# Modulation sums over partitions: quarters of the array, streamed, gathered by the group and turned once

## The chip, the cores and the metric

The kernel runs on one core of a Trainium2 chip. The metric is device time in microseconds of one execution, from the first to the last instruction with what the device adds around them; lower is better. Everything is fp32 at the interface. The engines are PE (matrix multiply), DVE (vector), ACT (activation), POOL (GpSimd) and SP, which issues the DMAs. Each engine works its own instructions in program order and waits on semaphores.

## The reference, cut to what matters

```python
for i in range(DEPTH):                       # DEPTH = 2, D_MODEL = 1024, 512 latent + 256 context tokens
    mx = (silu(c)     @ ada_w[i] + ada_b[i]).reshape(B, 1, 9, D_MODEL)   # for the latent tokens
    mc = (silu(c_ctx) @ ada_w[i] + ada_b[i]).reshape(9, D_MODEL)         # for the context tokens
    x   = x   + 0.5 * mx[2] * swiglu(modulate(rms_norm(x,   g), mx[0], mx[1]), w_gu, w_down)
    ctx = ctx + 0.5 * mc[2] * swiglu(modulate(rms_norm(ctx, g), mc[0], mc[1]), w_gu, w_down)
    ...                                      # i = 0: pooling and neighbourhood attention; i = 1: RG-LRU
    x   = x   + mx[5] * yx
    x   = x   + 0.5 * mx[8] * swiglu(modulate(rms_norm(x, g), mx[6], mx[7]), w_gu, w_down)
```

The change concerns the first two lines: two vectors of 1024 (silu of c and of c_ctx) times a matrix of 1024 x 9216 for each of the two layers. The 18432 results are the shifts, scales and gates of all stages that follow, for latent and for context tokens.

## The kernel before

The residual stream lies in SBUF with the channels on the partitions (8 tiles of 128 channels, 768 tokens in a row). Matmuls keep a 128x128 tile of a weight matrix in the array and stream the tokens. Each product is made of three passes: high part of the weights times high and low part of the tokens, low part times high. SP loads a weight panel (`raw`), ACT makes its high part (`w_hi`, L771), POOL the low one (`w_lo`, L661); there are two buffers of each, and a buffer is free when its panel has been used (`panel_used`).

An FFN f has two halves h. Stage `gu{f}{h}` makes gate and up products: 11 rounds of two panels (8 k-tiles each), into the PSUM tiles `pair_a` and `pair_b`, whence ACT takes silu and DVE makes g (L1090 to L1096). Stage `dn{f}{h}` multiplies g with `w_down`: 8 panels of 11 k-tiles, in turn into `pair_a` and `pair_b`, and DVE adds each, times its gate `mod_g`, to `resid` (L1121). Stages whose output is normed next (dn01, dn11 among them) end in a `tail` in which the last two panels are done by halves of the tokens. The order of the stages is gu00, dn00, gu01, dn01, then projections and attention, gu10, dn10, gu11, dn11, gu20, dn20, gu21, dn21, the recurrent block, and FFN 3.

The modulation is spread over these stages. The matrix is cut into 72 chunks of 256 columns. The first 8 are done in the prologue. The other 64 are done one by one: 11 in each of gu00, gu01, gu10, gu11 (one a round), 4 in each of dn00, dn01, dn10, dn11 and dn20 (one for every two panels). A chunk q goes like this:

- SP loads 1 MB of `ada_w` into `ada_raw` when the sums of chunk q-1 are done (`load_ada`, L508).
- DVE multiplies its 8 k-tiles with the two condition vectors and adds them up (`sum_ada`, L1056 and L1060, 16 instructions on 128x256), v = 0 for c and v = 1 for c_ctx. What is left is a sum over the 128 partitions of `ada_sum`.
- PE makes it (`use_ada`, L1648): for each tile t of 128 columns and each v the 128x128 block of `ada_sum` is the stationary operand and a column of ones the moving one. The result is one column of `pair_c`, with the channels already on the partitions.
- DVE adds the bias and stores two columns for each v in `mods` (`take_ada`, L1074). `mods_done` counts the chunks.

In a down stage DVE's order is: mod_g for the stage (`coef_g`, L1046), and then for each k from 0 to 7 `sum_ada` if k is even or `take_ada` if it is odd, the wait for panel k, the update of `resid`. PE calls `use_ada` behind panel 0, 2, 4 and 6. No scheduler is at work; the order on each engine is that of the code.

Of the kernel before, what the change touches and what calls it, by code (L numbers as in the profile page):

```python
# [91 lines left out]
HALF = T // 2  # L92
LEFT = 512 - HALF


def trunk(nc, x, c, ctx_in, c_ctx, ada_w, ada_b, norm_g, w_gu, w_down, ab_in, ab_out, pool_w,
# [51 lines left out]
    with ExitStack() as stack:  # L148
# [40 lines left out]
        ident = sb("ident", [P, P])  # L189
        ones = sb("ones", [P, P])  # L190
        rg_scale = sb("rg_scale", [P, 2 * KR])
        rg_tanh = sb("rg_tanh", [P, 2 * KR])
# [9 lines left out]
        acc = sb("sum_sq", [P, T])  # L202
        ada_sum = sb("ada_sums", [P, 2, 2 * P])

        def alias(start, end):
# [102 lines left out]
        ada_used = sem("ada_used")  # L308
        mods_done = sem("mods_done")
        coef_done = sem("coef_done")  # L310
        rows_landed = sem("rows_landed")
# [70 lines left out]
        def sums_before(q):  # L382

            return (q - ADA0) * (2 * KD)

        def ada_seen(q):
# [262 lines left out]
        def _(pool):  # L649
# [4 lines left out]
            nc.gpsimd.affine_select(out=ident[:, :], in_=ident[:, :], compare_op=ALU.not_equal, fill=1.0, base=0,  # L654
                                    pattern=[[-1, P]], channel_multiplier=1).then_inc(const_done, 1)

            def low(p, par, kt):
# [372 lines left out]
        def _(dve):  # L1030
# [32 lines left out]

            def sum_ada(q):

                dve.wait_ge(ada_landed, (q - (ADA0 - 1)) * 16)
                sum_tiles(lambda k: ada_raw[:, k, :], [ada_sum[:, v, :] for v in range(2)], ada_summed, sums_before(q))

            def take_ada(q):

                dve.wait_ge(ada_used, q - (ADA0 - 2))
                src = pC[:, 0:4].rearrange("p (t v) -> p v t", v=2)
                for v in range(2):
                    last = nc.vector.tensor_tensor(mods[:, ds(q * 2, 2), v], src[:, v, :], cols[:, ds(q * 2, 2)], ALU.add)  # L1074
                last.then_inc(mods_done, 1)

            def gate_up(f, h):
                W = SEQ if f == 3 else T
                p0, F0 = first[f"gu{f}{h}"], GU_BEFORE[f, h]
                q0 = ada_first.get(f"gu{f}{h}")  # L1080
                with dve.Fori(0, KC) as i:
                    if q0 is not None:
                        sum_ada(i + q0)
# [12 lines left out]
                    nc.vector.tensor_tensor(gl[:, ds(i, 1), 0:W].rearrange("p o n -> p (o n)"), gbuf[:, 0, 0:W],  # L1096
                                            gh[:, ds(i, 1), 0:W].rearrange("p o n -> p (o n)").bitcast(F32),
                                            ALU.subtract).then_inc(g_split_done, 1)
                    if q0 is not None:
                        take_ada(i + q0)  # L1100

# [28 lines left out]
            def outputs(name, p0):  # L1130

                site = SITE[name]
                if name[:2] != "dn" or name[3] == "0":
                    dve.wait_ge(mods_done, ada_seen((shift_tile(site) + 3 * KD) // 2 - 1))
# [3 lines left out]
                for k in range(KD - 2 if name in NORM_AT else KD):  # L1138
                    if q0 is not None:
# [72 lines left out]
            def tail(name, p0, q0):  # L1212

                i = NORM_AT[name]
                if q0 is not None:
                    sum_ada(q0 + KD // 2 - 1)
                dve.wait_ge(tail_mm, 2 * (i - 1) + 1)
# [6 lines left out]
                statistics(name, 0)  # L1224
                if q0 is not None:
                    take_ada(q0 + KD // 2 - 1)
                dve.wait_ge(panel_used, p0 + KD - 1)
# [14 lines left out]
                rows_of(name, 1, 0, KD)  # L1242
                if name == "dn01":
                    pad_tokens()

# [53 lines left out]


            dve.wait_ge(cols_t, 1)
            nc.vector.tensor_copy(cols[:, :], pR[:, 0:ROWS]).then_inc(cols_done, 1)
# [281 lines left out]
        def _(pe):  # L1584
# [56 lines left out]

            def use_ada(q):

                pe.wait_ge(ada_summed, sums_before(q + 1))
                pe.wait_ge(mods_done, q - (ADA0 - 1))
                for t in range(2):
                    for v in range(2):
                        last = nc.tensor.matmul(pC[:, 2 * t + v:2 * t + v + 1], ada_sum[:, v, t * P:(t + 1) * P],  # L1648
                                                ones[:, 0:1], start=True, stop=True)
                last.then_inc(ada_used, 1)  # L1650

            def gate_up(f, h, after):
                W = SEQ if f == 3 else T
                p0, F0 = first[f"gu{f}{h}"], GU_BEFORE[f, h]
                q0 = ada_first.get(f"gu{f}{h}")
                if after is not None:

                    first_panels(p0, after, W, W)
                    if q0 is not None:
                        use_ada(q0)  # L1660
                with pe.Fori(int(after is not None), KC) as i:
# [12 lines left out]
                    if q0 is not None:  # L1674
                        use_ada(i + q0)

            def outputs(name, p0, kt, hi, lo, start=0, each=None):
                W = SEQ if name in X_ONLY else T
                q0 = ada_first.get(name)
                with pe.Fori(start, KD // 2 - int(name in NORM_AT)) as i:  # L1680
                    for r in range(2):
                        pe.wait_ge(split_ready, i * 2 + (p0 + r + 1))

                        pe.wait_ge(resid_done, i * 2 + (UPD[name] + r - 1))
                        panel(pair[r], r, kt, hi, lo, W, each)
                        if q0 is not None and r == 0:
                            use_ada(i + q0)
                if name in NORM_AT:
# [21 lines left out]
            def tail(name, p0, kt, hi, lo, q0):  # L1710
# [12 lines left out]
                if q0 is not None:  # L1723
                    use_ada(q0 + KD // 2 - 1)
                half_panel(of[0], 0, kt, hi, lo, b, width(name), then(sum_rows, sum_at)).then_inc(panel_used, 1)
                half_panel(of[1], 1, kt, hi, lo, b, width(name), then(spread_rows, spread_at)).then_inc(panel_used, 1)

            def last_tile(n):
# [261 lines left out]
```

## Time and profile before

| | us |
|---|---|
| median of 3 runs (lowest, highest) | 2880.06 (2879.87, 2881.6) |
| profiled execution | 2877.64 |
| its span in the profile | 2875.9 |
| PE busy | 2719.7 (95%) |
| DVE busy | 1487.4 (52%) |
| ACT busy | 768.7 (27%) |
| POOL busy | 891.1 (31%) |
| mean granted clock of PE | 0.968 of full speed |

The span is what the profiler sees from the first to the last instruction; the profiled execution's own time is 1.7 us more. PE's matmuls overlap, and a record's length includes the way through the array, so the distance between two starts says more than the length of one record. An fp32 matmul shows as two records, the matmuls of the split products as one each. The clock is given as a share of 2.4 GHz; it is either 1.0 or 0.5 (1.2 GHz), and a stretch's figure is the mean.

### The profile page before, as it was taken

What the parts mean: (1) busy time and instruction counts of PE and PEld (TensorE: products, weight loads), DVE (VectorE), ACT (ScalarE), POOL (GpSimd) and SP (SyncE); (2) the same over time, 40 slices, a digit from 0 to 9 for tenths busy, and PEclk for the clock granted to TensorE, in tenths of its full rate; (3) what the DMA queues carried; (4) which work ended last, traced back from release to release, by engine and by line L of the source; (5) the groups of instructions that cost most, each with busy time, mean ns of one, the idle gap of its engine ahead of it and who ended that gap; (6) DMA issues with size and microseconds to landing.
All of it is one profiled execution on the core that took longest, in us unless ns stands there. A gap on an engine that the chain in (4) does not pass through costs nothing.

```text
span 2875.9 us, 40218 instructions
## 1 busy us (share of the span) xinstructions
PE 2719.7 (95%) x15161; PEld 2569.5 (89%) x15161; DVE 1487.4 (52%) x2553; ACT 768.7 (27%) x1039; POOL 891.1 (31%) x360
## 2 busy tenths in 40 slices
PE   6799999999998999999999999999998887899998
PEld 6799999998976899999999899999997775778887
DVE  5655555556545566546656423422248886432233
ACT  1322111112145322111112321111125664332222
POOL 0132223222233232322232222222323443344442
PEclk6899999999999999999999999999999998999999
DMA  5244434442220244434442123222211112233332
GB/s 200 64 126 126 115 90 126 125 120 63 59 78 27 59 117 117 131 96 117 117 131 82 52 66 101 81 59 66 75 46 51 48 47 66 62 94 103 88 103 80
DMA packets 413083, 256.77 MB, mean 89 GB/s; under 512 B 6653, under 2 KB 405846, under 8 KB 413014
## 3 DMA queue, kind: packets, MB, share of 16 engines
q1 hardware_dynamic: 413014, 255.87, 30.7%
q8 instruction: 40, 0.66, 0.1%
q14 instruction: 29, 0.24, 0.0%
HBM read 252.70 MB, written 4.25 MB: 89 GB/s over the span
## 4 chain that ended last, share of the span: by engine, by line
PE 64%; issue 20%; DVE 7%; POOL 5%; ACT 4%; DMA 0%; SPq 0%; POOLq 0%; DVEq 0%; ACTq 0%
PE pair_b L1598 29%; PE pair_a L1598 28%; POOL w_lo L661 5%; PE pair_c L1648 2%; DVE decay L1558 1%; DVE decay L1556 1%; DVE h_lo L1199 1%; PE pair_c L1849 1%; DVE gate_i L1552 1%; PE pair_a L1588 1%; DVE root L1550 1%; ACT root L1000 1%; ACT decay L998 1%; DVE ada_sums L1060 1%; PE pair_r L1867 1%
## 5 line engine op out<-in xcount | busy, mean ns | idle before, releaser
L661 POOL TENSOR_TENSOR w_lo<-raw,w_hi 128x1024 fp32r<-128x1024 f32 (+3 forms) x302 | 824.0, 2729 | 1796.0 <-ACT w_hi L771 1796.0
L771 ACT ACTIVATE w_hi<-raw 128x1024 fp32r<-128x1024 f32 (+3 forms) x302 | 337.2, 1117 | 1276.3 <-PE pair_b L1598 440.9
L1090 DVE TENSOR_TENSOR work_g<-work_s,pair_b 128x768 f32<-128x768 f32 (+1 forms) x88 | 78.1, 887 | 699.7 <-PE pair_b L1598 537.0
L1060 DVE SCALAR_TENSOR_TENSOR ada_sums<-ada_raw,cvec,ada_sums 128x256 f32<-128x256 f32 x896 | 395.5, 513 | 0.0
L1598 PE MATMUL pair_a<-h_hi,w_hi 128*128 128x384 f32 x1312 | 338.9, 339 | 9.7 <-POOL w_lo L661 9.6
L1598 PE MATMUL pair_a<-h_lo,w_hi 128*128 128x384 f32 x1312 | 334.2, 335 | 0.0
L1598 PE MATMUL pair_a<-h_hi,w_lo 128*128 128x384 f32 x1312 | 333.8, 335 | 0.0
L1598 PE MATMUL pair_b<-h_hi,w_hi 128*128 128x384 f32 x1168 | 297.3, 335 | 4.7 <-POOL w_lo L661 4.7
L1598 PE MATMUL pair_b<-h_lo,w_hi 128*128 128x384 f32 x1168 | 297.0, 335 | 0.0
L1598 PE MATMUL pair_b<-h_hi,w_lo 128*128 128x384 f32 x1168 | 296.8, 334 | 0.0
L1598 PEld LDWEIGHTS pair_a<-h_hi,w_hi 128*128 128x128 f32 x1312 | 234.7, 189 | 13.7 <-issue 9.6
L1598 PEld LDWEIGHTS pair_a<-h_lo,w_hi 128*128 128x128 f32 x1312 | 238.0, 189 | 0.0
L1598 PEld LDWEIGHTS pair_a<-h_hi,w_lo 128*128 128x128 f32 x1312 | 238.0, 188 | 0.0
L1598 PEld LDWEIGHTS pair_b<-h_hi,w_hi 128*128 128x128 f32 x1168 | 211.2, 188 | 5.3 <-POOL w_lo L661 5.3
L1598 PEld LDWEIGHTS pair_b<-h_hi,w_lo 128*128 128x128 f32 x1168 | 211.4, 188 | 0.0
L1598 PEld LDWEIGHTS pair_b<-h_lo,w_hi 128*128 128x128 f32 x1168 | 211.4, 188 | 0.0
L1121 DVE SCALAR_TENSOR_TENSOR resid<-pair_b,mod_g,resid 128x512 f32<-128x512 f32 (+3 forms) x74 | 42.2, 602 | 314.4 <-PE pair_b L1598 245.2
L1588 PE MATMUL pair_b<-h_hi,w_hi 128*128 128x512 f32 (+3 forms) x352 | 139.9, 397 | 33.6 <-DVE gelu L1537 33.4
L1096 DVE TENSOR_TENSOR g_lo<-work_g,g_hi 128x768 f32 (+1 forms) x88 | 161.5, 1835 | 10.8
L1589 PE MATMUL pair_b<-h_lo,w_hi 128*128 128x512 f32 (+3 forms) x352 | 137.5, 391 | 0.0
L1590 PE MATMUL pair_b<-h_hi,w_lo 128*128 128x512 f32 (+3 forms) x352 | 136.7, 388 | 0.0
L1588 PE MATMUL pair_a<-h_hi,w_hi 128*128 128x512 f32 (+2 forms) x280 | 115.3, 412 | 22.6 <-DVE h_lo L1199 18.7
(272 smaller groups left out, 4448.9 us busy)
## 6 DMA issues: line engine op xcount, KB each, us to landing
raw<-in_ffn_w_gu_dram SPq DMA_DIRECT2D x176, 512.0 KB, 3.9
ada_raw<-in_ada_w_dram SPq DMA_DIRECT2D x64, 1024.0 KB, 5.2
raw<-in_ffn_w_down_dram SPq DMA_DIRECT2D x64, 704.0 KB, 5.4
raw<-in_rg_w_in_dram SPq DMA_DIRECT2D x20, 512.0 KB, 3.8
ada_first<-in_ada_w_dram SPq DMA_DIRECT2D x4, 2048.0 KB, 17.9
raw<-in_ab_w_in_dram SPq DMA_DIRECT2D x16, 512.0 KB, 3.8
raw<-in_rg_w_out_dram SPq DMA_DIRECT2D x8, 640.0 KB, 4.5
raw<-in_ab_w_out_dram SPq DMA_DIRECT2D x8, 512.0 KB, 4.1
```

The costliest lines, as they stand in the source:

```text
L661: nc.gpsimd.tensor_tensor(wl[:, par, 0:kt * P], raw[:, par, 0:kt * P], wh[:, par, 0:kt * P].bitcast(F32), ALU.subtract).then_inc(split_rea ...
L771: nc.scalar.activation(wh[:, par, 0:kt * P], raw[:, par, 0:kt * P], ACT.Copy).then_inc(hi_done, 1)
L998: nc.scalar.activation(decay[d][:, :], gate_r[d][:, :], ACT.Exp, bias=rg_scale[:, m:m + 1], scale=rg_scale[:, m:m + 1])
L1060: step = nc.vector.scalar_tensor_tensor(out=sums[v], in0=tiles(k), scalar=c_k, in1=sums[v], op0=ALU.mult, op1=ALU.add)
L1090: nc.vector.tensor_tensor(gbuf[:, 0, 0:W], sbuf[:, 0, 0:W], up, ALU.mult)\
L1096: nc.vector.tensor_tensor(gl[:, ds(i, 1), 0:W].rearrange("p o n -> p (o n)"), gbuf[:, 0, 0:W], gh[:, ds(i, 1), 0:W].rearrange("p o n -> p ...
L1121: return nc.vector.scalar_tensor_tensor(out=resid[:, k, a:b], in0=src, scalar=mod_g[:, SITE[name], k, v:v + 1], in1=resid[:, k, a:b], op0= ...
L1588: nc.tensor.matmul(dst, w1, hi, start=start, stop=False)
L1589: nc.tensor.matmul(dst, w1, lo, start=False, stop=False)
L1590: return nc.tensor.matmul(dst, w2, hi, start=False, stop=stop)
L1598: last = nc.tensor.matmul(tokens(ps, a, a + HALF), w, of[:, k, a:a + HALF], start=begins, stop=ends)
L1648: last = nc.tensor.matmul(pC[:, 2 * t + v:2 * t + v + 1], ada_sum[:, v, t * P:(t + 1) * P], ones[:, 0:1], start=True, stop=True)
```

## The change

A chunk's four matmuls change sides. The block of `ada_sum` (128x128) now streams, and the stationary operand is `row_hot`, 128x32: ones in one of its 32 columns and zeros in the others. The four combinations of tile t and vector v go to the four column quarters c = 2t + v of the array, hence to partitions 32c to 32c+31 of `pair_c`, in 128 columns. The sum over partitions so comes out as one row of 128 values, in the row that `row_hot` selects; the other 31 rows get zeros added. DVE makes `row_hot` ahead of each chunk's sums by a copy of a window of `one_hot`, which moves the column of ones by one place with each chunk.

The chunks are gathered in six groups of 11, 15, 4, 11, 15 and 8 (GROUPS_AT). A group is opened by four matmuls of `one_hot` and `ident` with start=True (`begin_group`), its chunks accumulate without start, and at its end DVE copies the 128x128 result to `mod_rows` (`copy_group`), PE transposes it into the second bank of `pair_c` (`turn_group`), and DVE adds the biases for all its chunks with two instructions (`take_group`). Groups 0, 1, 3 and 4 are turned behind the first panel of dn00, dn01, dn10 and dn11, group 2 at the end of dn01, group 5 at the end of dn20. The first round of those four down stages is written out ahead of the loop. POOL fills `one_hot` in the prologue.

```diff
+        GROUPS_AT = [[("gu00", KC)], [("dn00", KD // 2), ("gu01", KC)], [("dn01", KD // 2)], [("gu10", KC)],
+                     [("dn10", KD // 2), ("gu11", KC)], [("dn11", KD // 2), ("dn20", KD // 2)]]
...
+        TURNED_IN = {"dn00": 0, "dn01": 1, "dn10": 3, "dn11": 4}
...
-            def sum_ada(q):
+            def sum_ada(q, name):
                 dve.wait_ge(ada_landed, (q - (ADA0 - 1)) * 16)
+                dve.wait_ge(ada_used, q - (ADA0 - 1))
+                nc.vector.tensor_copy(row_hot[:, :], one_hot[:, ds(q - GROUP_FIRST[GROUP_OF[name]], QUAD)]).then_inc(row_chosen, 1)
                 sum_tiles(lambda k: ada_raw[:, k, :], [ada_sum[:, v, :] for v in range(2)], ada_summed, sums_before(q))
 
-            def take_ada(q):
-                dve.wait_ge(ada_used, q - (ADA0 - 2))
-                src = pC[:, 0:4].rearrange("p (t v) -> p v t", v=2)
+            def copy_group(g):
+                dve.wait_ge(ada_used, ada_seen(GROUP_FIRST[g] + GROUP_SIZE[g] - 1))
+                nc.vector.tensor_copy(mod_rows[:, :], pC[:, 0:P]).then_inc(group_copied, 1)
+
+            def take_group(g):
+                q, n = GROUP_FIRST[g], GROUP_SIZE[g]
+                dve.wait_ge(group_turned, g + 1)
+                turned = pC[:, 640:640 + P].rearrange("p (t v j) -> p v t j", v=2, j=QUAD)[:, :, :, QUAD - n:QUAD]
                 for v in range(2):
-                    last = nc.vector.tensor_tensor(mods[:, ds(q * 2, 2), v], src[:, v, :], cols[:, ds(q * 2, 2)], ALU.add)
-                last.then_inc(mods_done, 1)
+                    last = nc.vector.tensor_tensor(mods[:, 2 * q:2 * (q + n), v].rearrange("p (j t) -> p t j", t=2),
+                                                   turned[:, v, :, ::-1],
+                                                   cols[:, 2 * q:2 * (q + n)].rearrange("p (j t) -> p t j", t=2), ALU.add)
+                last.then_inc(mods_done, n)
...
             def outputs(name, p0):                      # DVE
                 site = SITE[name]
+                if name in TURNED_IN:
+                    copy_group(TURNED_IN[name])
+                    take_group(TURNED_IN[name])
                 if name[:2] != "dn" or name[3] == "0":
...
                 for k in range(KD - 2 if name in NORM_AT else KD):
-                    if q0 is not None:
-                        if k % 2 == 0:
-                            sum_ada(q0 + k // 2)
-                        else:
-                            take_ada(q0 + k // 2)
+                    if q0 is not None and k % 2 == 0:
+                        sum_ada(q0 + k // 2, name)
                     dve.wait_ge(panel_used, p0 + k + 1)
...
+                if name == "dn20":
+                    copy_group(5)
+                    take_group(5)
...
+            def begin_group(g):                         # PE
+                if g == 0:
+                    pe.wait_ge(const_done, 5)
+                else:
+                    pe.wait_ge(group_copied, g)
+                for c in range(4):
+                    nc.tensor.matmul(pC[c * QUAD:(c + 1) * QUAD, 0:P], one_hot[:, QUAD:2 * QUAD], ident[:, :], start=True,
+                                     stop=False, skip_group_check=True)
+
+            def turn_group(g):
+                pe.wait_ge(group_copied, g + 1)
+                if g >= 1:
+                    pe.wait_ge(mods_done, ada_seen(GROUP_FIRST[g] - 1))
+                nc.tensor.transpose(pC[:, 640:640 + P], mod_rows[:, :], ident[:, :]).then_inc(group_turned, 1)
+
-            def use_ada(q):
+            def use_ada(q, name):
                 pe.wait_ge(ada_summed, sums_before(q + 1))
-                pe.wait_ge(mods_done, q - (ADA0 - 1))
+                pe.wait_ge(row_chosen, q - (ADA0 - 1))
                 for t in range(2):
                     for v in range(2):
-                        last = nc.tensor.matmul(pC[:, 2 * t + v:2 * t + v + 1], ada_sum[:, v, t * P:(t + 1) * P],
-                                                ones[:, 0:1], start=True, stop=True)
+                        c = 2 * t + v
+                        last = nc.tensor.matmul(pC[c * QUAD:(c + 1) * QUAD, 0:P], row_hot[:, :], ada_sum[:, v, t * P:(t + 1) * P],
+                                                start=False, stop=False, skip_group_check=True)
                 last.then_inc(ada_used, 1)
...
             def outputs(name, p0, kt, hi, lo, start=0, each=None):    # PE
...
                         panel(pair[r], r, kt, hi, lo, W, each)
+                        if opening and r == 0:
+                            if name in TURNED_IN:
+                                turn_group(TURNED_IN[name])
+                            if name in GROUP_OF and ada_first[name] == GROUP_FIRST[GROUP_OF[name]]:
+                                begin_group(GROUP_OF[name])
                         if q0 is not None and r == 0:
-                            use_ada(i + q0)
+                            use_ada(i + q0, name)
...
+                if name == "dn20":
+                    turn_group(5)
```

In the tail of a stage `take_ada` goes away too (dn01 has `copy_group(2)` in its place and `take_group(2)` at the end), and PE's `turn_group(2)` stands behind dn01's last half panel.

On DVE, at the end of gu00's loop and the opening of dn00, before (`mods` is the modulation, `mod_g` the gate of the stage, `ada_sums` the chunk's sums, `resid<-pair_a` the update with the first panel):

```order
L1074 TENSOR_TENSOR mods<-pair_c,cols 128x2
L1074 ISA
L1074 TENSOR_TENSOR mods<-pair_c,cols 128x2
L1081 REGISTER_ALU
L1081 COMPARE_AND_BRANCH
L1046 TENSOR_SCALAR mod_g<-mods 128x16
L1056 TENSOR_SCALAR ada_sums<-ada_raw,cvec 128x256 x2
L1060 SCALAR_TENSOR_TENSOR ada_sums<-ada_raw,cvec,ada_sums 128x256 x14
L1121 SCALAR_TENSOR_TENSOR resid<-pair_a,mod_g,resid 128x512
```

and now:

```order
L1095 COPY mod_rows<-pair_c 128x128
L1103 TENSOR_TENSOR mods<-pair_c,cols 128x2x11 x2
L1067 TENSOR_SCALAR mod_g<-mods 128x16
L1089 COPY row_hot<-one_hot 128x32
L1077 TENSOR_SCALAR ada_sums<-ada_raw,cvec 128x256 x2
L1081 SCALAR_TENSOR_TENSOR ada_sums<-ada_raw,cvec,ada_sums 128x256 x14
L1150 SCALAR_TENSOR_TENSOR resid<-pair_a,mod_g,resid 128x512
```

The chunk's two adds inside the loop are gone; between the loop and the next sums stand the copy out of PSUM, the adds of the whole group and the copy to `row_hot`.

On PE, around the end of dn00's first panel, before:

```order
L1598 MATMUL pair_a<-g_lo,w_hi 128x384 x2
L1598 MATMUL pair_a<-g_hi,w_lo 128x384 x2
L1644 ISA
L1648 MATMUL pair_c<-ones,ada_sums 128x1 x4
L1682 REGISTER_ALU
L1684 REGISTER_ALU
L1598 MATMUL pair_b<-g_hi,w_hi 128x384 x2
```

and now (`ident,mod_rows` is the turn, `ident,one_hot` the opening of group 1, `ada_sums,row_hot` the chunk):

```order
L1632 MATMUL pair_a<-g_lo,w_hi 128x384 x2
L1632 MATMUL pair_a<-g_hi,w_lo 128x384 x2
L1691 MATMUL pair_c<-ident,mod_rows 128x128
L1683 MATMUL pair_c<-ident,one_hot 32x128 x4
L1700 MATMUL pair_c<-ada_sums,row_hot 32x128 x4
L1632 MATMUL pair_b<-g_hi,w_hi 128x384 x2
```

The turn and four more matmuls stand between the panel and the chunk, and the chunk's matmuls have 128 moving columns on 32 columns of the array.

On DVE, at the end of dn20, now:

```order
L1150 SCALAR_TENSOR_TENSOR resid<-pair_b,mod_g,resid 128x512
L1150 SCALAR_TENSOR_TENSOR resid<-pair_b,mod_g,resid 128x256
L1095 COPY mod_rows<-pair_c 128x128
L1103 TENSOR_TENSOR mods<-pair_c,cols 128x2x8 x2
L1112 UNCONDITIONAL_BRANCH
```

The copy and the adds of group 5 stand behind the update with the last panel; before, nothing stood there, since the last chunk was taken ahead of that update.

## Rows read from the trace of the kernel before

**Rows 1.** the page, part 1: busy time, share of the span and instructions, by engine
```profile
PE 2719.7 (95%) x15161; PEld 2569.5 (89%) x15161; DVE 1487.4 (52%) x2553; ACT 768.7 (27%) x1039; POOL 891.1 (31%) x360
```

**Rows 2.** chain that ended last, 280 to 420 us: start, length, what, matmuls
```profile
by line: PE pair_b L1598 50.6%; PE pair_a L1598 45.5%; PE pair_c L1648 4.0%
...
300.24 0.94 PE pair_c L1648 x8
301.18 11.55 PE pair_b L1598 x66
```

**Rows 3.** PE's waits over the span: total us, times, longest us
```profile
PE pair_c L1648 <- DVE ada_sums L1060: 11.1, 5, 8.2
```

**Rows 4.** timeline of DVE, 286 to 316 us: start, length, instruction, [idle before]
```profile
287.94 0.95 DVE L1090 TENSOR_TENSOR work_g<-work_s,pair_b 128x768 f32<-128x768 f32 x1 [6.34 <-PE pair_b L1598]
...
290.60 0.22 DVE L1074 TENSOR_TENSOR mods<-pair_c,cols 128x2 f32 x2
290.74 0.17 DVE L1046 TENSOR_SCALAR mod_g<-mods 128x16 f32<-128x16 f32 x1
290.94 3.59 DVE L1056 TENSOR_SCALAR ada_sums<-ada_raw,cvec 128x256 f32<-128x256 f32 x2
294.45 5.62 DVE L1060 SCALAR_TENSOR_TENSOR ada_sums<-ada_raw,cvec,ada_sums 128x256 f32<-128x256 f32 x14
300.28 1.14 DVE L1121 SCALAR_TENSOR_TENSOR resid<-pair_a,mod_g,resid 128x512 f32<-128x512 f32 x2 [0.20 <-PE pair_a L1598]
```

**Rows 5.** timeline of PE, 299.4 to 302 us: start, length, instruction
```profile
299.73 0.51 PE L1598 MATMUL pair_a<-g_hi,w_lo 128*128 128x384 f32 x2
300.12 1.05 PE L1648 MATMUL pair_c<-ones,ada_sums 128*128 128x1 f32 x8
```

**Rows 6.** line 1648, all instances: duration ns min/median/max, first and last start us
```profile
L1648 PE MATMUL pair_c<-ones,ada_sums x512: 166/250/373, 104.7 to 1858.1; 128*128 128x1 f32 x171
```

**Rows 7.** timeline of PE around one chunk in gu00
```profile
147.47 0.95 PE L1648 MATMUL pair_c<-ones,ada_sums 128*128 128x1 f32 x8
148.28 0.59 PE L1598 MATMUL pair_a<-h_hi,w_hi 128*128 128x384 f32 x2
148.71 0.51 PE L1598 MATMUL pair_a<-h_lo,w_hi 128*128 128x384 f32 x2
149.06 0.33 PE L1598 MATMUL pair_a<-h_hi,w_lo 128*128 128x384 f32 x1
```

**Rows 8.** timeline of PE, 848.8 to 850.75 us: full width, halves, full width
```profile
848.89 0.76 PE L1849 MATMUL pair_c<-ident,prob 128*128 128x128 f32 x4
849.58 0.66 PE L1867 MATMUL pair_r<-prob_t,v_slabs 128*64 128x128 f32 x8
850.06 0.61 PE L1867 MATMUL pair_r<-prob_t,v_tokens 128*64 128x128 f32 x8
850.60 0.70 PE L1840 MATMUL pair_b<-k_t,q_t 64*128 64x512 f32 x2
```

**Rows 9.** timeline of PE's weight loads there
```profile
849.57 0.42 PEld L1867 LDWEIGHTS pair_r<-prob_t,v_slabs 128*64 128x64 f32 x8 [0.17 <-issue]
...
850.60 0.30 PEld L1840 LDWEIGHTS pair_b<-k_t,q_t 64*128 64x128 f32 x4 [0.17 <-DVE neg_max L1460]
```

**Rows 10.** line 1840, all instances: duration ns min/median/max
```profile
L1840 PE MATMUL pair_b<-k_t,q_t x48: 376/589/1220, 829.5 to 903.9; 64*128 64x512 f32 x32, 64*128 64x256 f32 x16
```

**Rows 11.** timeline of POOL, 285 to 322 us
```profile
291.04 3.33 POOL L661 TENSOR_TENSOR w_lo<-raw,w_hi 128x1408 fp32r<-128x1408 f32 x1 [6.02 <-ACT w_hi L771]
301.73 3.22 POOL L661 TENSOR_TENSOR w_lo<-raw,w_hi 128x1408 fp32r<-128x1408 f32 x1 [7.36 <-ACT w_hi L771]
```

**Rows 12.** stretches: length, PE busy (instructions), granted clock, DMA share, GB/s
```profile
99.50:104.70 5.20, 0.00 (x1) 0.50 0.00 0
104.70:109.80 5.10, 5.10 (x19) 0.50 0.78 245
...
119.90:123.40 3.50, 3.46 (x11) 0.52 1.12 354
```

More of the change, by code:

```diff
@@ L203, in trunk @@
         ada_sum = sb("ada_sums", [P, 2, 2 * P])
+        mod_rows = at("mod_rows", [P, P], F32, SBUF_END - size([P, P]))
+        row_hot = at("row_hot", [P, QUAD], F32, SBUF_END - size([P, P]) - size([P, QUAD]))
         def alias(start, end):
@@ L309, in trunk @@
         mods_done = sem("mods_done")
+        group_copied = sem("group_copied")
+        group_turned = sem("group_turned")
+        row_chosen = sem("row_chosen")
         coef_done = sem("coef_done")
@@ L384, in sums_before @@
             return (q - ADA0) * (2 * KD)
+        GROUPS_AT = [[("gu00", KC)], [("dn00", KD // 2), ("gu01", KC)], [("dn01", KD // 2)], [("gu10", KC)],
+                     [("dn10", KD // 2), ("gu11", KC)], [("dn11", KD // 2), ("dn20", KD // 2)]]
+        GROUP_OF, GROUP_FIRST, GROUP_SIZE = {}, [], []
+        for g, parts in enumerate(GROUPS_AT):
+            GROUP_FIRST.append(ada_first[parts[0][0]])
+            GROUP_SIZE.append(sum(n for _, n in parts))
+            for part, _ in parts:
+                GROUP_OF[part] = g
+        TURNED_IN = {"dn00": 0, "dn01": 1, "dn10": 3, "dn11": 4}
         def ada_seen(q):
@@ L655, in _ @@
                                     pattern=[[-1, P]], channel_multiplier=1).then_inc(const_done, 1)
+            nc.gpsimd.memset(one_hot[:, :], 0.0).then_inc(const_done, 1)
+            pool.wait_ge(const_done, 4)
+            nc.gpsimd.memset(one_hot[:, QUAD - 1:QUAD], 1.0).then_inc(const_done, 1)
             def low(p, par, kt):
@@ L1224, in tail @@
                 statistics(name, 0)
-                if q0 is not None:
-                    take_ada(q0 + KD // 2 - 1)
+                if name == "dn01":
+                    copy_group(2)
                 dve.wait_ge(panel_used, p0 + KD - 1)
@@ L1243, in tail @@
                 if name == "dn01":
+                    take_group(2)
                     pad_tokens()
@@ L1654, in gate_up @@
                 p0, F0 = first[f"gu{f}{h}"], GU_BEFORE[f, h]
-                q0 = ada_first.get(f"gu{f}{h}")
+                name = f"gu{f}{h}"
+                q0 = ada_first.get(name)
                 if after is not None:
@@ L1679, in outputs, with two @@
                 q0 = ada_first.get(name)
-                with pe.Fori(start, KD // 2 - int(name in NORM_AT)) as i:
+                def two(i, opening=False):
                     for r in range(2):
                         pe.wait_ge(split_ready, i * 2 + (p0 + r + 1))
-                        pe.wait_ge(resid_done, i * 2 + (UPD[name] + r - 1))
+                        if not isinstance(i, int) or i > 0 or r > 0 or UPD[name] > 0:
+                            pe.wait_ge(resid_done, i * 2 + (UPD[name] + r - 1))
                         panel(pair[r], r, kt, hi, lo, W, each)
-                        if q0 is not None and r == 0:
-                            use_ada(i + q0)
+                        if opening and r == 0:
+                            if name in TURNED_IN:
+                                turn_group(TURNED_IN[name])
+                            if name in GROUP_OF and ada_first[name] == GROUP_FIRST[GROUP_OF[name]]:
+                                begin_group(GROUP_OF[name])
+                        if q0 is not None and r == 0:
+                            use_ada(i + q0, name)
+                if name in TURNED_IN:
+                    two(0, True)
+                    start = 1
+                with pe.Fori(start, KD // 2 - int(name in NORM_AT)) as i:
+                    two(i)
+                if name == "dn20":
+                    turn_group(5)
                 if name in NORM_AT:
@@ L1723, in tail @@
                 if q0 is not None:
-                    use_ada(q0 + KD // 2 - 1)
+                    use_ada(q0 + KD // 2 - 1, name)
                 half_panel(of[0], 0, kt, hi, lo, b, width(name), then(sum_rows, sum_at)).then_inc(panel_used, 1)
                 half_panel(of[1], 1, kt, hi, lo, b, width(name), then(spread_rows, spread_at)).then_inc(panel_used, 1)
+                if name == "dn01":
+                    turn_group(2)
             def last_tile(n):
```

11 lines of the change are left out of this document (6 added, 5 removed).

## The prediction

> **What bounds the kernel now.** I read the page first, then the chain of waits, then the timeline around the line that the change rewrites. The page says PE is busy 95% of the span and DVE 52% [rows 1]. Busy PE is not proof, so the chain over 120 us of the first FFN follows: it is PE from end to end, 11.55 us for a panel of `w_down`, and between the panels the chunks of modulation sums at L1648, 4.0% of that stretch [rows 2]. So each microsecond that a chunk takes from PE is one of the kernel's, and each that PE waits there too. Last I looked at who is late for whom. L1648 waits for the sums of DVE (L1060) in five places, 11.1 us in all, of which 8.2 us is one wait at the start [rows 3]. At the opening of dn00 the two are level: the 16 sums begin at 290.94 and end at 300.07 (294.45 + 5.62), and PE takes them at 300.12 [rows 4, 5]. That is the place that I think decides this change.
>
> **The chunk itself.** 512 records on L1648 are 64 chunks of 4 fp32 matmuls, two records (high and low part) for each [rows 6]. One chunk: the records start at 147.47, the panel after it at 148.28, and that panel's first pair takes 0.43 us to the next instead of 0.35 [rows 7]. So 0.81 + 0.08 = 0.89 us, 57 us in all. With one moving column a record comes every 0.11 us (0.95 us for eight, the last 0.25 long), the pace of loading 128 columns of weights.
>
> Afterwards a chunk is again 4 matmuls and 8 records, but each streams 128 columns on one quarter of the columns. No row shows quarters; the nearest shows halves. L1867 (64 columns, 128 moving, fp32, the two heads on the two halves) does eight records in 0.61 us, the last 0.27 long [rows 8]: 0.34 us for three more pairs, so a pair every 0.11 us. A record holds its own columns for 0.11 us and the halves run together. With quarters the two records of each quarter take 0.22 us if all four run together, 0.44 us if only two do, 0.88 us if none.
>
> The array also has to change from full width to quarters and back. At 849 the last full-width record begins at 849.38 (848.89 + 0.76 - 0.27) and streams until 849.49; the first weights of the halves load only at 849.57, and those records are 0.05 us late (0.66 us for eight instead of 0.61), so matmuls begin at 849.63: 0.14 us, of which 0.08 is the change and the rest weights that nothing covers. For 32 columns I take half of that load: 0.12 us. Back (L1840 uses all columns again), the last record begins at 850.40 (850.06 + 0.61 - 0.27), is through at 850.51, weights load at 850.60, and the matmuls, 0.70 us for a median of 0.59, begin in effect at 850.71: 0.20 us [rows 8 to 10]. Sum for a chunk: 0.12 + 0.22 + 0.20 = 0.54 us, 0.35 less than now. **64 x 0.35 = 22.4 us gained.** Bounds: 0.22 us a chunk, with no cost of changing (43 us gained), and 0.12 + 0.88 + 0.20 = 1.20 us (20 us lost). I take the value of the row of halves, since it shows both the change of width and full overlap of what it has.
>
> The Trainium skill, "TensorE: Matmul & The Clock Gate", Part 3 (packing small matmuls), gives 2.38 times for three column tiles, so not a full threefold overlap; no run here has three. By it, as an estimate, four quarters would do about 3.2 times, a chunk would be 0.06 us longer and the gain 4 us less. The row of halves shows no such loss.
>
> **The openings of dn00, dn01, dn10 and dn11.** Here the change moves work. Before, DVE takes the last chunk, makes mod_g and starts the sums of the next chunk while PE is in the first panel. Now its queue reads: copy the group out of PSUM, add the turned group, mod_g, pick the row, and only then the sums. The add waits for `group_turned`, and PE turns only behind its first panel. Behind the turn PE opens the next group and then waits for those same sums. So 16 sums that the first panel hid stand in the open, and behind DVE's waiting add stand mod_g, the sums and the update of `resid`. From the end of the panel's stream (300.07, as 299.73 + 0.51 - 0.17):
> - the turn, one fp32 pass of 128 columns: 0.11 us
> - from PE to DVE: 0.21 us, as now (300.28) [rows 4]
> - add, mod_g, to the first sum: 290.60 to 290.94, 0.34 us; picking the row 0.15 us, like the small operation at L1074 (0.22 for two, overlapped)
> - the sums: 290.94 to 300.07, 9.13 us. Bare they would be 6.1 us; 3 us is one L1056 operation held while POOL makes w_lo (291.04, 3.33 us). The next w_lo runs 301.73 to 304.95, 7.36 us idle before it until ACT's w_hi, which that same panel's end releases, so it falls into the moved sums too [rows 4, 11]
> - DVE to PE: 0.05 us, which is there now as well.
> That is 9.9 us for dn00 and dn10, 9.7 us for dn01 and dn11 without mod_g: **39.3 us lost**. Opening the next group lies inside the wait. If POOL missed the sums it would be 27 us, the lower bound; POOL cannot hit them twice, as its next w_lo needs the next panel, so 43 us is the upper one. Nothing gives it back: the panels that follow are PE's own time, and the loads and w_lo for them are ahead in any case. The next load of ada_w on SP goes out 10 us later, but so does all that waits for it.
>
> **The clock.** In the one wait of this length, 8.2 us from 96.5, the granted clock went to half (1.2 GHz) within the wait and stayed there from 104.70 to 109.80, with PE working: 5.1 us at half, 2.5 us lost. At 119.90, after another wait of PE, it was 3.5 us at half, 1.7 us lost [rows 3, 12]. Four waits at the mean of both, 2.1 us: **8.4 us lost**, between 6.8 and 10.
>
> **The rest.** At the end of dn20 PE turns the last group and must wait until DVE has updated `resid` with the last panel and copied the group; today PE goes on without a gap there. DVE starts 0.21 us behind the panel, the update takes 1.14 us [rows 4], the copy of 128x128 I put at 0.27 us (between the 0.15 us of L1074 and 0.39 us, the second part of that update), then two weight loads and the turn, 0.2 us: **1.8 us**. The turn at the end of dn01 and opening the groups at gu00 and gu10: 0.6 us at most. DVE's small operations in the gate/up loops (one copy for two adds) lie in idle time of 6.3 us a turn [rows 4], and POOL's two memsets in the prologue's waiting: nothing. If that cover went, it would be 0.15 us a chunk.
>
> **Sum.** -22.4 + 39.3 + 8.4 + 1.8 + 0.6 = +27.7 us on the profiled execution's 2877.64 us (its span of 2875.9 plus 1.7 around it): 2905.3. The median of the runs shown, 2880.06, is 2.4 above that execution, so **2908 us**, 1.0% slower.
>
> **The rivals.**
> - Quarters in pairs: no row shows four streams into one bank at once, and none forbids it. A chunk is 0.76 us, the gain 8 us instead of 22: 2922. One after another (1.20 us): 2950. These are also the cases in which the change fails to do what it says.
> - Cheaper chunks: the full-width stream goes on under the quarters, with no cost of changing, 0.22 us each. Against it stands the 0.17 us of idle weight loading at each change in rows 9. Gain 43: 2887.
> - Faster, by one mechanism: the first sums of the four down stages are not held by the turn. Then PE has no new wait and keeps its clock, and what remains is -22.4 + 1.8 + 0.6 = -20 us: 2860. The place is DVE's queue at the opening; it decides as soon as a wait costs, with its clock, less than 5 us (20 divided by four). For it: today the two are level there to 0.05 us. Against it: DVE works its queue in order, the add stands ahead of the sums, and the bare sums alone are 6.1 us.
> - Sums that POOL doesn't touch, and shorter clock losses: 27 + 6.8 instead of 39.3 + 8.4: 2894.
>
> **How the numbers follow.** The forecast, with its own range 2899 to 2917, gets 66%; pairs 12%, serial 5%; cheaper chunks 7%; POOL missing the sums 5%; the faster one 5%. From 2893 to 2928 leaves out the serial case, the faster one and part of the cheap chunks. A difference under 0.2% (5.8 us) can't be told from none here. Slower 0.92, same 0.03 (cheap chunks and bare sums together), faster 0.05.
>
> **What would show it.** Right: on PE four waits of 9 to 10 us at the modulation matmuls for DVE's sums, each right behind the first panel of dn00, dn01, dn10 and dn11; a granted clock of 0.5 behind each for 3 to 5 us; DVE's idle time before the add of the turned group, for PE's turn; chunks elsewhere 0.54 us from stream to stream; a gap of under 2 us at the end of dn20. Wrong: PE waits there under 5 us; or a chunk of 0.76 us or more, which is the pairs; or sums of 6.1 us behind the turn.

## The result and the profile after

The changed kernel takes 2908.16 us (median of 4 runs, 2906.58 to 2910.49), the kernel before 2880.13 in the same comparison: 1.0097 times as long, 95% interval 1.0079 to 1.0114. It is slower by 28 us. The profiled execution has a span of 2905.9 us, 30.0 more than before. One execution of pool_waits, an experiment below, took 5298.4 us against 2900.5 in the median of its five others, and is left out of its figures.

First the page, part 1 (busy time by engine), to be held against [rows 1]:

```profile
PE 2709.3 (93%) x15215; PEld 2530.2 (87%) x15215; DVE 1488.4 (51%) x2507; ACT 768.8 (26%) x1039; POOL 895.1 (31%) x362
```

PE is busy for 10 us less and the span is 30 us longer, so most of what was lost is waiting (work at a lower clock counts as busy, so its cost lies hidden in the first figure). PE's waits (total, times, longest) name it; [rows 3] had 11.1 us on this line:

```profile
PE pair_c L1700 <- DVE ada_sums L1081: 47.2, 9, 9.4
```

DVE's waits have a new line too, for the turned group:

```profile
DVE mods L1103 <- PE pair_c L1691: 36.8, 5, 9.2
```

The opening of dn00 on DVE (start, length, instruction, idle before), which answers to [rows 4]:

```profile
289.65 0.28 DVE L1095 COPY mod_rows<-pair_c 128x128 f32<-128x128 f32 x1
299.12 0.28 DVE L1103 TENSOR_TENSOR mods<-pair_c,cols 128x22 f32<-128x22 f32 x2 [9.19 <-PE pair_c L1691]
...
299.74 0.61 DVE L1077 TENSOR_SCALAR ada_sums<-ada_raw,cvec 128x256 f32<-128x256 f32 x2
300.27 8.52 DVE L1081 SCALAR_TENSOR_TENSOR ada_sums<-ada_raw,cvec,ada_sums 128x256 f32<-128x256 f32 x14
```

Before, the sums began at 290.94, under the first panel. Now DVE copies the group at 289.65, then sits idle for 9.19 us until the turn, and the sums run from 299.74 to 308.79. The same place on PE, answering to [rows 5]:

```profile
298.47 0.51 PE L1632 MATMUL pair_a<-g_hi,w_lo 128*128 128x384 f32 x2
298.81 0.27 PE L1691 MATMUL pair_c<-ident,mod_rows 128*128 128x128 f32 x1
299.01 0.42 PE L1683 MATMUL pair_c<-ident,one_hot 128*32 128x128 f32 x8
308.84 0.66 PE L1700 MATMUL pair_c<-ada_sums,row_hot 128*32 128x128 f32 x8 [9.40 <-DVE ada_sums L1081]
309.42 1.01 PE L1632 MATMUL pair_b<-g_hi,w_hi 128*128 128x384 f32 x2
310.23 0.84 PE L1632 MATMUL pair_b<-g_lo,w_hi 128*128 128x384 f32 x2
```

The panel's stream ends at 298.81 (298.47 + 0.51 - 0.17), turn and opening of the group follow, and the chunk starts at 308.84: 10.0 us behind the panel, where it was 0.05 us. The next pairs of matmuls come 0.64 us to 0.81 us apart instead of 0.35: the clock. Stretches behind the four waits, PE busy and granted clock, to be held against [rows 12]:

```profile
308.80:314.30 5.50, 5.46 (x23) 0.50 0.81 244
...
604.30:607.90 3.60, 3.60 (x18) 0.50 0.60 193
...
1228.70:1232.50 3.80, 3.80 (x18) 0.50 0.66 210
...
1523.40:1529.50 6.10, 6.10 (x25) 0.50 0.87 255
```

One chunk in gu00 on PE, answering to [rows 7], and its weight loads:

```profile
148.63 0.51 PE L1632 MATMUL pair_b<-h_hi,w_lo 128*128 128x384 f32 x2
149.07 0.43 PE L1700 MATMUL pair_c<-ada_sums,row_hot 128*32 128x128 f32 x8
149.42 0.62 PE L1632 MATMUL pair_a<-h_hi,w_hi 128*128 128x384 f32 x2
149.88 0.52 PE L1632 MATMUL pair_a<-h_lo,w_hi 128*128 128x384 f32 x2
150.24 0.52 PE L1632 MATMUL pair_a<-h_hi,w_lo 128*128 128x384 f32 x2
```

```profile
149.07 0.16 PEld L1700 LDWEIGHTS pair_c<-ada_sums,row_hot 128*32 128x32 f32 x8 [0.25 <-issue]
149.42 0.30 PEld L1632 LDWEIGHTS pair_a<-h_hi,w_hi 128*128 128x128 f32 x2 [0.20 <-issue]
```

Eight records take 0.43 us where they took 0.95. Cutting the window to the first 0.08 us leaves this row:

```profile
149.07 0.32 PE L1700 MATMUL pair_c<-ada_sums,row_hot 128*32 128x128 f32 x4
```

Four records span 0.32 us, and one such record is 0.27 to 0.30 us long, so all four began within some 0.03 us: the quarters do run side by side.

**Where the 30 us are.** The main matmuls are the same in both kernels, so the starts of chunks serve as marks in both traces (us):

| chunk | before | after | difference |
|---|---|---|---|
| 2nd of gu00 | 129.94 | 131.84 | +1.90 |
| last of gu00 | 287.74 | 286.88 | -0.86 |
| 2nd of dn00 | 324.00 | 334.77 | +10.77 |
| last of gu01 / 2nd of dn01 | 575.86 / 612.00 | 582.64 / 629.32 | +6.78 / +17.32 |
| last of gu10 / 2nd of dn10 | 1191.86 / 1228.10 | 1206.86 / 1253.84 | +15.00 / +25.74 |
| last of gu11 / 2nd of dn11 | 1479.95 / 1516.10 | 1501.71 / 1549.55 | +21.76 / +33.45 |
| last of dn20 | 1857.44 | 1889.25 | +31.81 |
| end of the span | 2875.9 | 2905.9 | +30.0 |

Nine rounds of gu00 gain 2.76 us, 0.307 us a chunk, 19.6 us for 64. The four openings cost 11.63 + 10.54 + 10.74 + 11.69 = 44.6 us net of the two chunks that lie in each, so 47.1 us without them. With 2 us at the end of dn20 (below) that makes +29.5. What is left lies in three other stretches: +1.9 us before the second chunk, +1.7 us between dn01 and gu10 (beside the chunks' own gain), and -3.5 us behind dn20. They cancel. The last has no edit. The first two also hold the openings of groups 0 and 3 and the turn of group 2, but 1.4 us of the first is a longer wait of PE for POOL's w_lo (4.8 us instead of 3.4).

### The profile page after: what moved, and what is told of

The parts are those of the page before. It is cut to its first block, busy times and chain, and to the rows that moved or that the text cites. A ratio compares the mean times of both kernels' runs of the same rounds, so it can differ in the third digit from the quotient of the medians.

```text
span 2905.9 us, 40208 instructions
## 1 busy us (share of the span) xinstructions
PE 2709.3 (93%) x15215; PEld 2530.2 (87%) x15215; DVE 1488.4 (51%) x2507; ACT 768.8 (26%) x1039; POOL 895.1 (31%) x362
## 4 chain that ended last, share of the span: by engine, by line
PE 63%; issue 20%; DVE 8%; POOL 5%; ACT 4%; DMA 0%; SPq 0%; POOLq 0%; DVEq 0%; ACTq 0%
PE pair_b L1632 29%; PE pair_a L1632 28%; POOL w_lo L682 5%; DVE ada_sums L1081 2%; DVE decay L1592 1%; PE pair_c L1700 1%; DVE decay L1590 1%; PE pair_c L1921 1%; DVE gate_i L1586 1%; DVE h_lo L1231 1%; DVE root L1584 1%; ACT root L1021 1%; ACT decay L1019 1%; PE pair_r L1939 1%; PE pair_a L1622 1%
## 5 line engine op out<-in xcount | busy, mean ns | idle before, releaser
L1081 DVE SCALAR_TENSOR_TENSOR ada_sums<-ada_raw,cvec,ada_sums 128x256 f32<-128x256 f32 x896 | 404.1, 523 | 0.0
L1127 DVE TENSOR_TENSOR g_lo<-work_g,g_hi 128x768 f32 (+1 forms) x88 | 130.9, 1487 | 10.8
L1622 PE MATMUL pair_a<-h_hi,w_hi 128*128 128x512 f32 (+2 forms) x280 | 114.5, 409 | 23.3 <-DVE h_lo L1231 19.6
```

The costliest lines, as they stand in the source:

```text
L1081: step = nc.vector.scalar_tensor_tensor(out=sums[v], in0=tiles(k), scalar=c_k, in1=sums[v], op0=ALU.mult, op1=ALU.add)
L1622: nc.tensor.matmul(dst, w1, hi, start=start, stop=False)
```

## The experiments

twice, one_quarter, full_width and old_one_of_four change or leave out part of the modulation, as told with each; the others compute all of it. Times are medians; the ratio is to the kernel before, run on the same chip beside each. They come from three comparisons, in which the kernel before has medians from 2880.2 to 2881.6 us, so a difference of 1 or 2 us between two rows says nothing.

| kernel | us | ratio | 95% interval |
|---|---|---|---|
| sums_first | 2866.09 | 0.9949 | 0.9936 to 0.9962 |
| old_late_sums | 2923.89 | 1.0156 | 1.0143 to 1.0169 |
| pool_waits | 2900.51 | 1.0067 | 1.0054 to 1.0080 |
| keep_busy | 2901.33 | 1.0078 | 1.0065 to 1.0091 |
| copy_early | 2862.79 | 0.9936 | 0.9921 to 0.9950 |
| twice | 2880.86 | 1.0001 | 0.9992 to 1.0010 |
| one_quarter | 2903.52 | 1.0079 | 1.0064 to 1.0095 |
| full_width | 2887.46 | 1.0028 | 1.0018 to 1.0038 |
| old_one_of_four | 2845.09 | 0.9873 | 0.9858 to 0.9888 |

The profiles separate the openings from all else. The four stretches from the last chunk before an opening to the second chunk of it take together:

| kernel | us | against before |
|---|---|---|
| before | 144.8 | |
| after | 189.4 | +44.6 |
| sums_first | 143.2 | -1.6 |
| old_late_sums | 192.8 | +48.0 |
| pool_waits | 177.4 | +32.6 |
| keep_busy | 180.9 | +36.1 |

**sums_first: the order alone undone.**

```diff
                     copy_group(TURNED_IN[name])
+                    sum_ada(ada_first[name], name)
                     take_group(TURNED_IN[name])
...
-                    if q0 is not None and k % 2 == 0:
+                    if q0 is not None and k % 2 == 0 and not (k == 0 and name in TURNED_IN):
```

> The changed kernel with DVE's first sums of dn00, dn01, dn10 and dn11 moved ahead of the add that waits for the turn. Theory (the four openings lose the time by DVE's order): the four waits of 9.4 us and the half clock behind them go, 47 us less the four turns and openings of groups, some 0.4 us each: 2908 - 45 = 2863, faster than the kernel before by 17 us, which is the chunks' own gain. Rival (turns, openings of groups and changes of width cost the time, the wait only shows it): PE's waits go and the time stays above 2890.

Measured 2866.1: 42 us less than the changed kernel and 0.5% faster than the one before. The rival is out. PE at the opening of dn00:

```profile
298.66 0.51 PE L1633 MATMUL pair_a<-g_hi,w_lo 128*128 128x384 f32 x2
299.01 0.27 PE L1692 MATMUL pair_c<-ident,mod_rows 128*128 128x128 f32 x1
...
299.45 0.40 PE L1701 MATMUL pair_c<-ada_sums,row_hot 128*32 128x128 f32 x8
299.78 0.62 PE L1633 MATMUL pair_b<-g_hi,w_hi 128*128 128x384 f32 x2
```

Turn, opening of the group and chunk follow each other without a wait, and the next panel begins 0.78 us behind the end of the last one (299.00). The quarters and the gathering were sound; where the sums stood was not.

**old_late_sums: the order alone, in the kernel before.**

```diff
+                        if k == 0 and name in ("dn00", "dn01", "dn10", "dn11"):
+                            dve.wait_ge(panel_used, p0 + 1)
                         if k % 2 == 0:
                             sum_ada(q0 + k // 2)
```

> The kernel before with one wait more: in those four stages DVE begins the first sums only when PE has used the first panel. Theory: this alone costs what the openings cost in the changed kernel, less the turn and the small operations on DVE, 0.11 + 0.5 us each: 4 x (9.1 + 0.2 + 2.1) = 46 us less 0.2, about 2925. Rival (the order costs little without the quarters and the turn): below 2900.

Measured 2923.9, 42 us over the kernel before beside it; the rival is out. PE's wait:

```profile
PE pair_c L1650 <- DVE ada_sums L1060: 47.3, 9, 9.3
```

With neither quarters nor groups the kernel has the same 47 us of waiting on this line as the changed one (47.2). The loss belongs to the order of DVE's queue.

**pool_waits: POOL kept off the moved sums.** The changed kernel, and in POOL's queue behind the second panel's w_lo of each of the four stages:

```diff
+                low(p0, 0, KC)
+                low(p0 + 1, 1, KC)
+                pool.wait_ge(ada_summed, sums_before(ada_first[name] + 1))
+                pairs(p0, 1, KD // 2, KC)
```

> The changed kernel, with POOL's w_lo of the third panel of those four stages held until the first sums are done. Theory (3 us of each wait is one DVE operation held while POOL works): the waits fall from 9.4 to 6.4 us, 12 us less, 2896, and up to 4 us less again if the clock stays up longer. Rival (the sums are slow behind the turn for another reason): the same 2908.

DVE at the opening of dn00:

```profile
301.21 0.28 DVE L1114 TENSOR_TENSOR mods<-pair_c,cols 128x22 f32<-128x22 f32 x2 [9.19 <-PE pair_c L1702]
...
301.83 0.61 DVE L1088 TENSOR_SCALAR ada_sums<-ada_raw,cvec 128x256 f32<-128x256 f32 x2
302.35 5.63 DVE L1092 SCALAR_TENSOR_TENSOR ada_sums<-ada_raw,cvec,ada_sums 128x256 f32<-128x256 f32 x14
```

The sums take 6.15 us (301.83 to 307.98) instead of 9.05, and PE's waits on the line fell by 11.6 us:

```profile
PE pair_c L1711 <- DVE ada_sums L1092: 35.6, 9, 8.1
```

So the operation that is held while POOL works is worth 2.9 us at each opening, and the rival is out. The shorter wait didn't save the clock: behind it PE again worked at half, at dn00 until about 311.7 (the mean of 0.60 in the second row is 0.5 for 1.3 us and 1.0 for the rest).

```profile
308.10:310.30 2.20, 2.20 (x13) 0.50 0.42 94
310.40:312.00 1.60, 1.60 (x7) 0.60 1.09 387
```

Behind the four waits PE worked at half for 3.6, 5.5, 3.5 and 5.5 us, 18.1 us in all, where it was 19.0 in the changed kernel: the further gain of up to 4 us that was expected from the clock came to some 0.4. The four openings are 12.0 us shorter than in the changed kernel (189.4 to 177.4), as expected from the waits. The whole time fell by less, 7.7 us by the medians (2908.2 to 2900.5, which are of two comparisons) and 5.6 us from span to span. In the profiles the difference lies outside the openings: 2 us were there before the first one (DVE takes the turned group at 301.21 here, at 299.12 in the changed kernel) and 3 us behind dn20, where nothing was changed; what made them isn't known.

**keep_busy: PE at work in the wait.**

```diff
                                 begin_group(GROUP_OF[name])
+                            for _ in range(40):
+                                nc.tensor.matmul(pR[:, 0:P], ones[:, :], ident[:, :], start=True, stop=True)
```

> The changed kernel, with 40 more 128x128 fp32 matmuls into an idle bank behind the opening of the group in those four stages, 8.6 us, so that PE works while DVE sums. Theory (half clock behind the wait costs 2 us each time): the granted clock stays 1.0 there and the time falls by 8 us to 2900. Rival (the clock falls whatever PE does there, or the matmuls outlast the sums): the same or slower, 2908 to 2912.

Measured 2901.3, 7 us less than the changed kernel by the medians; the intervals of the two ratios overlap, so the trace has to show it. On PE, and its clock through wait and restart:

```profile
298.07 9.20 PE L1749 MATMUL pair_r<-ident,ones 128*128 128x128 f32 x80
307.55 0.42 PE L1700 MATMUL pair_c<-ada_sums,row_hot 128*32 128x128 f32 x8 [0.28 <-DVE ada_sums L1081]
307.91 0.62 PE L1632 MATMUL pair_b<-g_hi,w_hi 128*128 128x384 f32 x2
308.37 0.52 PE L1632 MATMUL pair_b<-g_lo,w_hi 128*128 128x384 f32 x2
```

```profile
304.00:308.00 4.00, 3.72 (x39) 1.00 0.01 4
308.00:312.00 4.00, 4.00 (x23) 1.00 0.81 260
```

The chunk comes as late as before, 10.0 us behind the panel (297.51 to 307.55), but the granted clock stays at 1.0 (2.4 GHz) and the next pair is 0.46 us behind the first instead of 0.81. The four openings are 8.5 us shorter than in the changed kernel (189.4 to 180.9). The clock's part of the openings is real and apart from the wait's.

**copy_early: the end of dn20.** sums_first, and:

```diff
+                    if name == "dn20" and k == KD - 2:
+                        copy_group(5)
...
                 if name == "dn20":
-                    copy_group(5)
                     take_group(5)
```

> sums_first, with DVE's copy of the last group in dn20 ahead of its update with the last panel instead of behind it. Theory (PE waits 1.6 us at the end of dn20 for update and copy): 1.5 to 2 us less than sums_first in the same comparison, the gap gone from the trace. Rival (the next stage waits for that update anyway): no difference between the two traces at that place. By the median the difference is near what can be told.

The changed kernel there, then copy_early:

```profile
1900.84 0.51 PE L1632 MATMUL pair_b<-g_hi,w_lo 128*128 128x384 f32 x2
1902.78 0.33 PE L1691 MATMUL pair_c<-ident,mod_rows 128*128 128x128 f32 x1 [1.43 <-DVE mod_rows L1095]
1903.17 0.59 PE L1632 MATMUL pair_a<-h_hi,w_hi 128*128 128x384 f32 x2
```

```profile
1856.08 0.51 PE L1634 MATMUL pair_b<-g_hi,w_lo 128*128 128x384 f32 x2
1856.42 0.27 PE L1693 MATMUL pair_c<-ident,mod_rows 128*128 128x128 f32 x1
1856.45 0.59 PE L1634 MATMUL pair_a<-h_hi,w_hi 128*128 128x384 f32 x2
```

From the panel's last pair to the next stage it was 2.33 us and is 0.37 us: 2 us gone. The medians, 2866.1 and 2862.8, can't confirm it: the spread of each is as large as the difference, they are of two comparisons, and the two spans are 2861.4 and 2861.5. This version has the lowest median, 0.6% under the kernel before, but isn't shown to be faster than sums_first.

**twice, one_quarter, full_width: what a chunk is made of.** All three are sums_first with `use_ada` changed. twice issues each matmul a second time, so the sums are doubled; one_quarter has all four on quarter 0, where they mix; full_width has the identity as the stationary operand over all 128 columns, so nothing is summed over partitions.

```diff
-                        c = 2 * t + v
+                        c = 0                                             # one_quarter
...
-  nc.tensor.matmul(pC[c * QUAD:(c + 1) * QUAD, 0:P], row_hot[:, :], ada_sum[:, v, t * P:(t + 1) * P], ...)
+  nc.tensor.matmul(pC[:, 0:P], ident[:, :], ada_sum[:, v, t * P:(t + 1) * P], ...)   # full_width
```

> sums_first with each chunk's four quarter matmuls issued twice, so that the modulation sums come out doubled. Theory (four quarters stream together, 0.22 us for four fp32 matmuls, and the other 0.37 us of a chunk is the change of width there and back): each chunk grows by 0.22 us, 14 us more than sums_first, 2880. Rival (a chunk is mainly its matmuls, the changes are cheap): 0.5 us a chunk, 32 us more, 2898.

> sums_first with all four matmuls of a chunk on the first quarter of the columns, so that all land in the same rows and most sums are wrong. Theory (quarters run side by side): now one after another, 8 x 0.107 instead of 0.22 us, 0.64 us more a chunk, 41 us more than sums_first, 2907. Rival (the side by side is only how the records are written): under 10 us more.

> sums_first with each of a chunk's four matmuls over the full width, the identity as the stationary operand and the 128 columns of sums streaming, so that the modulation is wrong. Against one_quarter (which streams as long, one after another) only the change of width is gone. Theory (about 0.35 us of a chunk is the change there and back): 0.86 us a chunk instead of 1.22, 17 us more than sums_first, 2883, and 20 us less than one_quarter. Rival (that rest belongs to fp32 matmuls behind the split products, or to their weights): the same as one_quarter, 2903.

A chunk in gu00 in each, in this order, and the matmuls behind it:

```profile
168.74 0.65 PE L1701 MATMUL pair_c<-ada_sums,row_hot 128*32 128x128 f32 x16
169.33 0.61 PE L1633 MATMUL pair_a<-h_hi,w_hi 128*128 128x384 f32 x2
```

```profile
167.68 1.06 PE L1701 MATMUL pair_c<-ada_sums,row_hot 128*32 128x128 f32 x8
168.67 0.61 PE L1633 MATMUL pair_a<-h_hi,w_hi 128*128 128x384 f32 x2
```

```profile
166.87 1.05 PE L1701 MATMUL pair_c<-ada_sums,ident 128*128 128x128 f32 x8
167.67 0.59 PE L1633 MATMUL pair_a<-h_hi,w_hi 128*128 128x384 f32 x2
```

From the chunk's first record to the panel: 0.35 us in the changed kernel, 0.59 twice, 0.99 on one quarter. The second set of four costs 14.8 us by the medians, 0.23 us a chunk, near the 0.22 expected (they are of two comparisons; by the rows above it is 0.24). On one quarter it is 37 us in all, 0.58 us a chunk by the medians and 0.64 by the rows: four streams that had run side by side now queue. Both rivals are out. full_width streams for as long as one_quarter and is 16 us faster (20 expected). A round of gu00 is 17.53 us long in it and 17.85 us on one quarter (chunks at 167.68 and 185.53), so the change of width there and back is worth 0.32 us of a chunk. The 17.53 us of full_width (chunks at 166.87 and 184.40) are those of the kernel before (147.47 and 165.00). So in these rounds letting the sums stream instead of a column of ones is worth nothing by itself; all of the chunk's gain is the quarters'.

**old_one_of_four.** The kernel before with range(1) in both loops of `use_ada`; three quarters of the sums are missing.

> The kernel before with one of a chunk's four matmuls, so that three quarters of the sums are missing. Theory (each fp32 matmul with one column costs two weight loads of 0.112 us, in a row with all else): 6 x 0.112 = 0.67 us less a chunk, 43 us in all, 2838. Rival (part of a chunk is a fixed cost of leaving the panel's stream): less than 30 us.

```profile
167.27 0.28 PE L1648 MATMUL pair_c<-ones,ada_sums 128*128 128x1 f32 x2
167.41 0.60 PE L1598 MATMUL pair_a<-h_hi,w_hi 128*128 128x384 f32 x2
```

The chunk's two records and the way to the panel take 0.14 us instead of 0.81, the expected 0.67 us, and the rounds of gu00 are shorter by as much (16.87 us against 17.53). But the median fell by 36 us and not by 43. Part of the rest is seen: at the openings PE now arrives first. Its waits for the sums are nine instead of five, 2 us more in all:

```profile
PE pair_c L1648 <- DVE ada_sums L1060: 13.1, 9, 8.2
```

A PE that is faster in the loops finds DVE's sums late at an opening even in the old order. The four openings are 2.5 us shorter than in the kernel before, where eight chunks at 0.67 us would make 5.3: 2.8 of the missing 7 us. The prologue of this trace also ran 3 us later; whether the other executions did isn't known, and the rest stays open. The rival (under 30) is out.

## Why the prediction was right

It gave 2908 us and 2908.2 were measured. The mechanism is the one that was forecast, and each large term holds to 3 us or better; that the end figure holds to 0.2 us is luck, as the last paragraph shows.

- The chunk: forecast 0.54 us and a gain of 22.4, measured 0.59 (0.89 - 0.307) and 19.6. Weights load 0.10 us behind the stream's end (148.97 to 149.07) and the first records are 0.02 us longer than the others, which makes the 0.12 of the way in; the array is at work for 0.24 us instead of 0.22; the way back is 0.20 as forecast. The error is in the streams, 0.02 us, and in the first pairs afterwards, which come 0.36 us apart instead of 0.35 (149.88 to 150.24), some 0.03. The row of halves [rows 8] was the right one to size quarters by. The Trainium skill's 2.38 times for three column tiles ("TensorE: Matmul & The Clock Gate", Part 3), from which the prediction made 3.2 times for four, was near too: from the first start to the last it is 0.79 us on one quarter and 0.16 us on four (1.06 and 0.43, each less 0.27), and with 0.11 us for the last stream that makes 0.90 against 0.27, 3.3 times.
- The wait: forecast 39.3 us. From the end of the panel's stream to the chunk it was 10.0 us at dn00, 9.7 at dn01, 9.9 at dn10 and 9.7 at dn11, 39.3 in all and 39.2 more than before. DVE had the turned group 0.31 us behind the panel (forecast 0.32), its first sum 0.62 us later (0.49), and the sums took 9.05 us (9.13), 2.9 us of it through POOL. old_late_sums and sums_first show that DVE's order is the cause: put into the kernel before, it makes the openings longer (+48.0 us); taken out of the changed one, it leaves them 1.6 us shorter than before.
- The clock: forecast 8.4 us. Behind the waits PE worked 5.5 + 3.6 + 3.8 + 6.1 = 19.0 us at half, so 9.5 us lost at most; 47.1 less 39.2 of waiting leaves 7.9; the openings of keep_busy are 8.5 us shorter. The term was right to 1 us. The forecast took the wait of 8.2 us for the only one of its length; the trace before has another, of 10.0 us for POOL's w_lo at 2400.6, behind which PE worked at half for 3.1 us (2410.6 to 2413.7), in line with the term.
- The end of dn20: forecast 1.8 us, measured 2.0 (2.33 less 0.37).
- The rest: the turn at the end of dn01 and the openings of groups 0 and 3, 0.6 us at most by the forecast, lie in the two stretches that are 1.9 and 1.7 us longer, and can't be told there from what else changes.

So 22.4 was 3 us too much on the gain's side, and the losses were right to 1 us in sum. That the median was met to 0.2 us is more than the terms deserve. The sum gave 2905.3 for the profiled execution, which took 2907.6; and to it were added 2.4 us from that execution to the median, where it was 0.5 this time. Two errors of 2 us cancel, and the three other stretches, +1.9, +1.7 and -3.5 us, which the forecast did not have, cancel too. The rival on the other side, sums that the turn does not hold, was a true account of another kernel: it gave 2860 with the wait of dn20 still in, and sums_first, which is that kernel, took 2866.1. The rival gave 20 us won and it was 15; 3 of the difference are the chunks.

## What to carry to other kernels

Where a step is gathered and taken later, look at what stood behind the old step in the consumer's queue: here a wait for PE's turn was put ahead of work that PE itself needs 10 us later, and one line moved turns 28 us lost into 15 won. Price a wait with its length and with the clock behind it. Sending narrow matmuls to column quarters has to pay for the change of width there and back: here 0.32 us a visit, against 0.63 us that running side by side saved (17.85 us a round on one quarter, 17.23 on four).

## What the runs showed of the hardware

- Four fp32 matmuls of 128x32 with 128 moving columns on four quarters begin within 0.03 us and take about 0.24 us together; one after another on one quarter they take 0.64 us more.
- A change from full width to quarters and back around one chunk costs 0.32 us (rounds of 17.85 and 17.53 us).
- A chunk's four fp32 matmuls at full width cost the same with 1 moving column and with 128: the round is 17.53 us either way.
- PE kept at work with 128-column fp32 matmuls for 9.2 us kept its granted clock at 1.0. Waits of 6.2 to 6.5 us cost the clock nearly as much as waits of 9.1 to 9.4: PE then worked 3.5 to 5.5 us at half in the one case, 3.6 to 6.1 us in the other.
- One of DVE's sums that meets POOL's w_lo is held for 2.9 us (9.05 us for 16, 6.15 without).
